# Mixing phase with an early stage eight tiles ahead, 16x16 inverses on VectorE, and the output product in fp16 halves

## Chip, core and metric

One NeuronCore of a Trainium2 chip runs the whole kernel. The metric is the device time of one execution in microseconds. Times inside the run are taken from one profiled execution and count from its first instruction.

## What is computed

The kernel is one inference step of a one-layer encoder over 4096 prompt tokens and 8 running streams of 16 tokens, 33 tiles of 128 tokens in all, D = 1024. A layer is: RMSNorm and one input projection; an RG-LRU group and a gated-DeltaNet group of 4 heads side by side; one output projection and a residual; RMSNorm and a routed mixture of 32 experts (2 per token); a last RMSNorm. The change lies in the DeltaNet group and the output projection:

```python
decay = exp(where(lower, gc[..., :, None] - gc[..., None, :], -inf))
lmat = where(strict, einsum('bhid,bhjd->bhij', k * beta, k) * decay, 0.0)
t_inv = triangular_solve(eye + lmat, eye, lower=True, unit_diagonal=True)
u = t_inv @ (v * beta[..., None])
w = t_inv @ (k * beta * exp(gc)[..., None])
v_new = u - w @ S
o = (q * exp(gc)[..., None]) @ S + (einsum('bhid,bhjd->bhij', q, k) * decay) @ v_new
S_new = S * exp(g_last) + einsum('bhld,bhle->bhde', k * exp(g_last - gc), v_new)
...
mixed = concatenate([out_a, rmsnorm(o, gdn_ng) * silu(z)])
x = x + mixed @ w_out
```

S is carried from tile to tile, so the tiles have an order; t_inv of a tile needs only its own k, beta and decay.

## The kernel before

Five phases run one after the other: projection (all inputs of the mixing go to the DRAM tensor `mixin`), mixing, routing, experts, combine. Only mixing is touched.

Mixing (`mix_phase`) walks over the 33 tiles; the last one holds the streams. The work of a tile is cut into named steps, each on one engine, in three stages: X (what doesn't need S: row sums `stat`, decay `dec`/`DT`, the products `KK` and `QK`, the matrix G, and the inverse of the 128x128 triangle), Y (what needs S: `KS`, `QS`, `X`, `N`, `dS`, `AV`, the head norm `so`/`ro`/`on`, the output product `outA`/`outB`) and R (residual `x2`, second norm `st`/`r2`/`xn`, router `hT`/`lg`/`r0` to `r3`, rank `rk`/`off` and the scatter `sct`).

The list `MIX` (L645 to 669) gives the order by hand: `name.engine` from top to bottom. Each engine runs its own steps in that order (`program`, L799), waiting for the steps it needs by semaphores; one pass of the list does R of tile t, Y of tile t+1 and X of tile t+2, and the loop holds two passes. So a step that waits holds back all that stand behind it on its engine.

The inverse doubles its block size seven times (1, 2, 4, ... 64, `LEVELS`). A level s is: `Bs` on GpSimd (G times a mask), `Ws` on TensorE (L919), `Is` on VectorE (plus identity, L1247), `Ts` on TensorE (L929), its copy `Tsc` on ScalarE (L1070), the transpose `Zs` (L935) and its copy `Zsc` (L1078); level 1 is done on VectorE (`Z1`). Each product is four heads of 128x128 in fp32, which are eight TensorE instructions, a transpose four. The steps `outA0` to `outA3` (two chunks of 128 each, L998) and `outB0` to `outB7` (one head each, L1010) multiply by `w_out` in fp32, 512 columns at a time, and are spread between the levels.

On SP (SyncE's queue) stands one load of the tile's inputs `ft` and one of `xr` per tile (L830, L832). ScalarE issues the stores of x2 and h2, GpSimd the two scatters of `sct` (L1174), each followed by a wait for its landing.

Of the kernel before, what the change touches and what calls it, by code (L numbers as in the profile page):

```python
# [13 lines left out]
FP32 = mybir.dt.float32  # L14
# [24 lines left out]
LEVELS = [1, 2, 4, 8, 16, 32, 64]  # L39
# [4 lines left out]
PROJ = 1.0 / (W_SCALE * H_SCALE)  # L44
G_SCALE = 4.0
# [17 lines left out]
MATS = ["ident", "upto", "after", "upto_s", "after_s", "before", "ones"] + [f"level{s}" for s in LEVELS]  # L63
# [582 lines left out]
X.sq.act X.gs.dve  # L646
Y.KS.pe Y.QS.pe Y.X.dve R.x2.dve Y.o1.act R.st.act R.r2.pool
X.stat.pe X.dec.pe X.sse.dve X.ex.act X.DT.act X.rr.pool R.xn.dve R.h2.pool
Y.N.pe Y.vd.dve Y.vh.act
X.kt.pe X.ktc.act X.vt.pe X.sc.dve  # L650
R.hT0.pe R.hT1.pe R.hc0.dve R.hc1.dve
Y.dS.pe Y.S.dve Y.AV.pe
X.KK.pe X.QK.pe X.vs.act X.G.dve X.B2.pool X.Z1.dve Y.o.dve X.AT.dve
R.lg.pe Y.so.act Y.ro.pool R.r0.dve
Y.outA2.pe X.B4.pool
X.T1.pe X.T1c.act R.r1.dve R.rx.act Y.on.dve
Y.outA3.pe X.ATm.pool
X.W2.pe X.I2.dve Y.outA0.pe
X.T2.pe X.T2c.act Y.outA1.pe Y.oT.pe X.B8.pool
X.W4.pe X.Z2.pe X.Z2c.act Y.mx.dve X.I4.dve Y.outB0.pe X.B16.pool  # L660
X.T4.pe X.T4c.act Y.outB1.pe X.B32.pool
X.W8.pe X.Z4.pe X.Z4c.act R.hh.act X.I8.dve R.r3.dve Y.outB2.pe
X.T8.pe X.T8c.act Y.outB3.pe X.B64.pool
X.W16.pe X.Z8.pe X.Z8c.act X.I16.dve R.hl.dve R.rk.pe
X.T16.pe X.T16c.act Y.outB4.pe R.off.dve
X.W32.pe X.Z16.pe X.Z16c.act X.I32.dve Y.outB5.pe R.sct.pool
X.T32.pe X.T32c.act Y.outB6.pe
X.W64.pe X.Z32.pe X.Z32c.act R.sh.act X.I64.dve Y.outB7.pe
X.Z64.pe X.Z64c.act
# [5 lines left out]
def mix_phase(nc, T, gb, cols, eid, rank, wts, base):  # L675
    NT = tiles()
    H = HEADS
    with ExitStack() as ctx:
# [3 lines left out]
        def sem(name):  # L682
# [3 lines left out]
        w_out = sb("w_out", [P, KD, D])  # L686
# [4 lines left out]
        xr = [sb(f"xr{p}", [P, D]) for p in range(2)]  # L691
        sqb = sb("sqb", [P, 2 * H, P])
# [30 lines left out]
        junk = sb("junk2", [P, D])  # L723
# [75 lines left out]
        def program(engine, begin, x_step, y_step):  # L799

            for (st, e), d in done.items():
                if e == engine:
                    d.begin(begin)

            def run(x, y, r):
                for st, n, e in MIX:
                    tile = {"X": x, "Y": y, "R": r}[st]
                    if e == engine and tile is not None:
                        (x_step if st == "X" else y_step)(n, tile[0], tile[1], tile[2], done[st, e].did)

            last = NT - 1
            run((0, 0, False), None, None)
            run((1, 1, False), (0, 0, False), None)
            with begin.Fori(0, (last - 2) // 2) as pair:
                t = pair * 2
                run((t + 2, 0, False), (t + 1, 1, False), (t, 0, False))
                run((t + 3, 1, False), (t + 2, 0, False), (t + 1, 1, False))
            run((last, 0, True), (last - 1, 1, False), (last - 2, 0, False))
            run(None, (last, 0, True), (last - 1, 1, False))
            run(None, None, (last, 0, True))  # L820
# [1189 lines left out]
```

## Time and profile before

| | us |
|---|---|
| median of 3 runs | 4321.36 |
| lowest, highest | 4320.52, 4328.91 |
| the profiled execution | 4329.62 |
| its span, first to last instruction | 4328.0 |
| TensorE busy | 3577.7 (83%) |
| VectorE busy | 2200.0 (51%) |
| ScalarE busy | 1679.3 (39%) |
| GpSimd busy | 947.6 (22%) |
| mean granted TensorE clock | 0.927 of 2.4 GHz |

A line of the order of time gives the start, the time from the first instruction's start to the last one's end, the engine, the line of the kernel, the operation and its tiles; in brackets how long the engine stood idle before it and who released it. Ends of TensorE instructions are modelled and overlap the next start, so the distance between starts tells what a group occupies. The granted clock is a share of 2.4 GHz; 0.50 is 1.2 GHz.

### The profile page before, as it was taken

The page shows a single profiled execution, that of the slowest core. Times are in us where ns is not written, and L with a number is a line of the kernel's source. Part 1 is how long each engine was busy: PE and PEld are TensorE (multiplying, and loading weights), DVE is VectorE, ACT ScalarE, POOL GpSimd, SP SyncE. Part 2 cuts the span into 40 slices and gives each one's busy share as a digit, 9 for nine tenths or more (in the row PEclk, how much of TensorE's full clock was granted, in tenths as well). Part 3 has the DMA queues.
Part 4 walks back from the last instruction along what each step waited for, and adds up shares of the span by engine and source line. Part 5 has one row for each costly group of instructions (what it writes and reads, how often), then busy time and mean ns, then how long its engine had stood idle before and what let it go on. Part 6 is the DMA issues. An engine that isn't in the chain of part 4 may idle for free. (4 is left out here: it accounts for less than half of the span.)

```text
span 4328.0 us, 72419 instructions
## 1 busy us (share of the span) xinstructions
PE 3577.7 (83%) x21028; PEld 2176.8 (50%) x21029; DVE 2200.0 (51%) x4880; ACT 1679.3 (39%) x2974; POOL 947.6 (22%) x1046
## 2 busy tenths in 40 slices
PE   8987696886978589899989999998739999999920
PEld 3443343333434567666766766676524444444410
DVE  6566474664756445655655565556432222222257
ACT  6556465564655433333333333333112222222222
POOL 0000000000000123333333334333111111111145
PEclk9998898998989699999999999999869999999965
DMA  4465656656565312121112111221046666774379
GB/s 146 150 207 195 223 191 216 213 198 212 196 202 190 131 35 68 53 65 58 63 53 65 58 63 54 64 68 54 15 185 225 224 231 220 271 269 151 107 293 381
DMA packets 293079, 656.24 MB, mean 152 GB/s; under 512 B 26467, under 2 KB 138595, under 8 KB 292579
## 3 DMA queue, kind: packets, MB, share of 16 engines
q1 hardware_dynamic: 182162, 321.70, 23.4%
q0 software_dynamic: 56512, 186.76, 11.5%
q10 hardware_dynamic: 54288, 146.56, 8.7%
q14 instruction: 85, 0.69, 0.1%
q8 instruction: 32, 0.52, 0.1%
HBM read 404.57 MB, written 250.38 MB: 151 GB/s over the span
## 5 line engine op out<-in xcount | busy, mean ns | idle before, releaser
L341 PE MATMUL pP<-h_hi,w_hi 128*128 128x512 f16 (+1 forms) x1728 | 634.8, 371 | 59.4 <-ACT win L435 40.1
L341 PE MATMUL pP<-h_lo,w_hi 128*128 128x512 f16 (+1 forms) x1728 | 634.6, 371 | 0.0
L341 PE MATMUL pP<-h_hi,w_lo 128*128 128x512 f16 (+1 forms) x1728 | 632.8, 370 | 0.0
L1631 PE MATMUL ebank<-ws_sb,rowsT 128*128 x2352 | 528.3, 382 | 40.0 <-issue 39.0
L1631 PEld LDWEIGHTS ebank<-ws_sb,rowsT 128*128 128x128 f16 x2352 | 229.4, 98 | 313.7 <-issue 67.6
L542 DVE SCALAR_TENSOR_TENSOR halves<-stage,halves 128x1024 f16<-128x1024 f32 x192 | 234.5, 1222 | 248.5 <-ACT halves L411 248.5
L293 POOL DMA_DIRECT2D ws<-halves x192 | 103.2, 537 | 1122.1 <-DVE halves L542 615.8
L577 DVE SCALAR_TENSOR_TENSOR cv<-win,cols_sb,cv 128x512 f32<-128x512 f32 (+1 forms) x432 | 305.5, 707 | 33.9 <-issue 0.9
L1247 DVE TENSOR_TENSOR WI<-bank,const 128x512 f32<-128x512 f32 x198 | 136.5, 690 | 351.6 <-PE bank L919 347.1
L341 PEld LDWEIGHTS pP<-h_hi,w_hi 128*128 128x128 f16 x1728 | 174.3, 101 | 256.2 <-ACT win L435 44.6
L411 ACT ACTIVATE halves<-stage 128x1024 f16<-128x1024 f32 x192 | 201.9, 1052 | 259.8 <-POOLq L296 255.7
L1144 POOL TENSOR_TENSOR B<-G,const 128x512 f32<-128x512 f32 x198 | 255.9, 1313 | 139.0 <-DVE G L1228 133.3
L1649 PE MATMUL ebank<-ws_sb,guT 128*128 x1176 | 269.9, 379 | 2.4 <-DVE guT L1705 2.4
L919 PEld LDWEIGHTS bank<-Tm,B 128*128 128x128 f32 x1584 | 196.7, 195 | 146.9 <-ACT Tm L1070 78.4
L1010 PE MATMUL bank<-w_out,mx 128*128 128x512 f32 x528 | 269.6, 594 | 0.8 <-DVE mx L1309 0.8
L341 PEld LDWEIGHTS pP<-h_lo,w_hi 128*128 128x128 f16 x1728 | 174.1, 101 | 190.5 <-issue 19.9
L341 PEld LDWEIGHTS pP<-h_hi,w_lo 128*128 128x128 f16 x1728 | 174.6, 101 | 187.7 <-issue 11.3
L919 PE MATMUL bank<-Tm,B 128*128 128x128 f32 x1584 | 229.9, 290 | 34.6 <-ACT Tm L1066 30.7
L998 PE MATMUL bank<-w_out,ft 128*128 128x512 f32 x528 | 251.0, 599 | 0.0
L929 PE MATMUL bank<-WI,Zm 128*128 128x128 f32 x1320 | 198.1, 295 | 61.5 <-DVE WI L1247 47.6
L929 PEld LDWEIGHTS bank<-WI,Zm 128*128 128x128 f32 x1320 | 167.0, 199 | 156.4 <-DVE WI L1247 84.7
L1700 DVE SCALAR_TENSOR_TENSOR gu<-ebank,sil 128x256 f32<-128x256 f32 x98 | 41.6, 425 | 392.0 <-ACT sil L1668 392.0
(290 smaller groups left out, 6036.3 us busy)
## 6 DMA issues: line engine op xcount, KB each, us to landing
stage<-in_we SPq DMA_DIRECT2D x192, 512.0 KB, 4.1
ws<-halves POOLq DMA_DIRECT2D x192, 512.0 KB, 3.9
ws_sb<-ws SPq DMA_DIRECT2D x32, 3072.0 KB, 13.7
y<-yb ACTq DMA_DIRECT2D x98, 512.0 KB, 4.7
ft<-mixin SPq DMA_DIRECT2D x33, 1280.0 KB, 6.1
mixin<-qo ACTq DMA_DIRECT2D x128, 256.0 KB, 2.8
xt<-in_x SPq DMA_DIRECT2D x33, 512.0 KB, 5.9
xr<-in_x SPq DMA_DIRECT2D x33, 512.0 KB, 4.8
```

The costliest lines, as they stand in the source:

```text
L341: ins = nc.tensor.matmul(pP[n % NPB][:, 0:N], w[:, k, c0:c0 + P], h[:, k, 0:N], start=(k + i == 0), stop=(k == KD - 1 and i == 2))
L411: nc.scalar.activation(halves[:, j % 2, 0, :], stage[:, j % 2, :, :].rearrange("p k n -> p (k n)"), ACT.Copy, scale=W_SCALE).then_inc(expe ...
L542: nc.vector.scalar_tensor_tensor(halves[:, j % 2, 1, :], stage[:, j % 2, :, :].rearrange("p k n -> p (k n)"), W_SCALE, halves[:, j % 2, 0, ...
L577: ins = nc.vector.scalar_tensor_tensor(dst, window(c, j, stream), cw(j), dst, ALU.mult, ALU.add)
L919: ins = nc.tensor.matmul(XB[:, h, :], Bs[s][:, h, :], Tm[:, h, :], start=True, stop=True)
L929: ins = nc.tensor.matmul(XC[:, h, :], Zm[:, h, :], WI[:, h, :], start=True, stop=True)
L998: ins = nc.tensor.matmul(flat((YD, YE)[half]), ft[p][:, QC + ZC + c, :], w_out[:, c, half * 512:half * 512 + 512], start=(c == 0), stop=False)
L1010: nc.tensor.matmul(flat((YD, YE)[half]), mx[:, h, :], w_out[:, LC + h, half * 512:half * 512 + 512], start=False, stop=(h == H - 1)).then_ ...
L1144: nc.gpsimd.tensor_tensor(Bs[s][:, :, :], G[:, :, :], heads(mat(f"level{s}")), ALU.mult).then_inc(*did(n))
L1247: nc.vector.tensor_tensor(WI[:, :, :], XB[:, :, :], heads(mat("ident")), ALU.add).then_inc(*did(n))
L1631: ins = nc.tensor.matmul((M0, M1)[p][:, :], xT[p][:, x, k, :], half(s, k // 2, w, k % 2 * 512), start=(k + i == 0), stop=(k == KD - 1 and ...
L1649: ins = nc.tensor.matmul((OA, OB)[h][:, :], guT[p][:, x, k, :], half(pe_slot[0], W13 // WC + k, w, h * 512), start=(k + i == 0), stop=(k = ...
```

## The change

A fourth stage F is added: `sq`, `gs`, `stat`, `dec`, `KK`, `QK`, G, the scalars `fsc` and the masked `AT` of a tile are made eight tiles ahead (`LEAD`), from q and k loaded on their own (`qk`), and kept in DRAM (`Gs`, `As`, the 16x16 diagonal blocks of G in `Gd`) or in `st_all`. Once in four tiles a step `V` on VectorE inverts the diagonal blocks of four tiles at once: 4 tiles x 4 heads x 8 blocks lie on the 128 partitions (`va`), 15 steps of a product and a subtraction, in two parts in two passes. The results go to DRAM (`Td`, `Zd`) and come back as `Tin` and `Zin`, which GpSimd spreads into block diagonals (`eT`, `eZ`). The levels 1 to 8 go; 16, 32 and 64 stay. The output product takes w_out and both factors as fp16 high and low halves, three fp16 products for one in fp32 (`split_out`, `fh`/`fl`, `mh`/`ml`). A pass now does R of tile i-1, Y of i, X of i+1, F of i+8; the loop holds four passes, from -8 to 33 with those outside the loop.

```diff
 MIX = """
-(18 rows, X, Y and R as above)
+Y.KS.pe Y.QS.pe Y.X.dve R.x2.dve Y.o1.act R.st.act X.eT.pool X.B16.pool X.eZ.pool R.r2.pool
+X.kt.pe X.vt.pe X.sc.dve X.ktc.act F.gs.dve F.sq.act
+Y.N.pe Y.vd.dve Y.vh.act X.vs.act R.xn.dve
+F.stat.pe F.sse.dve F.ex.act F.rr.pool X.B32.pool
+Y.dS.pe Y.AV.pe Y.S.dve
+R.hT0.pe R.hT1.pe R.hc0.dve R.hc1.dve Y.o.dve R.h2.pool
+X.W16.pe X.I16.dve F.dec.pe F.DT.act
+R.lg.pe F.fsc.dve R.r0.dve Y.so.act Y.ro.pool R.hh.act
+X.T16.pe X.T16c.act F.KK.pe F.G.dve X.B64.pool
+Y.outA0.pe X.Z16.pe X.Z16c.act R.r1.dve R.rx.act
+X.W32.pe X.I32.dve Y.outA1.pe Y.on.dve
+X.T32.pe X.T32c.act F.QK.pe F.AT.dve Y.oT.pe F.ATm.pool
+X.Z32.pe X.Z32c.act Y.mx.dve Y.mh.act X.W64.pe X.I64.dve Y.outA2.pe Y.ml.dve
+X.Z64.pe X.Z64c.act Y.outA3.pe R.r3.dve R.sh.act
+Y.outB0.pe Y.outB1.pe R.rk.pe V.v.dve R.hl.dve R.off.dve R.sct.pool
+Y.outB2.pe Y.outB3.pe Y.outB4.pe Y.outB5.pe Y.outB6.pe Y.outB7.pe X.fh.act X.fl.dve
 """.split()
...
+            def early_store(f):
+                sp.wait_ge(*at("G", f))
+                for b in range(NB16):
+                    r = slice(b * BW, (b + 1) * BW)
+                    sp.dma_start(T["Gd"][bass.ds(f, 1), :, b].rearrange("a h i j -> i (a h) j"), G[r, :, r]
+                                 ).then_inc(diag_out, 16)
+                sp.dma_start(T["Gs"][bass.ds(f, 1)].rearrange("a p h n -> p (a h) n"), G[:, :, :]).then_inc(G_out, 16)
+                sp.wait_ge(*at("ATm", f))
+                sp.dma_start(T["As"][bass.ds(f, 1)].rearrange("a p h n -> p (a h) n"), ATf[:, :, :]).then_inc(AT_out, 16)
...
+            def load(t, p, batches):
+
                 sp.wait_ge(*at("mx", t, 2))
                 sp.dma_start(ft[p][:, :, :], T["mixin"][:, :, bass.ts(t, P)]).then_inc(ft_in[p], 16)
-                sp.wait_ge(*at("x2", t, 2))
-                sp.dma_start(xr[p][:, :], T["x"][bass.ts(t, P), :]).then_inc(xr_in[p], 16)
+                sp.wait_ge(*at("B64", t, 1))
+                sp.dma_start(Gin[:, :, :], T["Gs"][bass.ds(t, 1)].rearrange("a p h n -> p (a h) n")).then_inc(G_in, 16)
+                sp.wait_ge(*at("AV", t, 2))
+                sp.dma_start(AT[p][:, :, :], T["As"][bass.ds(t, 1)].rearrange("a p h n -> p (a h) n")).then_inc(AT_in[p], 16)
+                sp.wait_ge(inverse_out, batches * 32)
+                for dst, src, there in ((Tin, "Td", T_in), (Zin, "Zd", Z_in)):
+                    sp.dma_start(dst[p][:, :, :], T[src][bass.ds(t, 1)].rearrange("a h k i j -> (k i) (a h) j")
+                                 ).then_inc(there[p], 16)
...
                 elif n[:-1] == "outA":
...
                     for c in (2 * c0, 2 * c0 + 1):
-                        ins = nc.tensor.matmul(flat((YD, YE)[half]), ft[p][:, QC + ZC + c, :],
-                                               w_out[:, c, half * 512:half * 512 + 512], start=(c == 0), stop=False)
+                        for i, (w, f) in enumerate(((w_out_hi, f_hi), (w_out_lo, f_hi), (w_out_hi, f_lo))):
+                            ins = nc.tensor.matmul(flat((YD, YE)[half]), f[:, c, :],
+                                                   w[:, c, half * 512:half * 512 + 512], start=(c + i == 0), stop=False)
...
+                if n in ("eT", "eZ"):
+                    pool.wait_ge(*at("W16" if n == "eT" else "T16", t, 1))
+                    pool.wait_ge((T_in if n == "eT" else Z_in)[p], ft_turn(t, p))
...
+                    for h in range(H):
+                        ins = nc.gpsimd.tensor_tensor(whole[:, h, :].rearrange("p (k j) -> p k j", k=NB16),
+                                                      small[:, h, :].unsqueeze(1).to_broadcast([P, NB16, BW]), same, ALU.mult)
...
+            def inversion(b, part):
...
+                for k in range(0, 7) if part == 0 else range(7, BW - 1):
+                    n, c = BW - 1 - k, k + 1
+                    prod = vp[:, 0:n * c].rearrange("p (n c) -> p n c", n=n)
+                    nc.vector.tensor_tensor(prod, va[:, k, k + 1:].unsqueeze(2).to_broadcast([P, n, c]),
+                                            vt_[:, k, 0:c].unsqueeze(1).to_broadcast([P, n, c]), ALU.mult)
+                    dve.drain()
+                    nc.vector.tensor_tensor(vt_[:, k + 1:, 0:c], vt_[:, k + 1:, 0:c], prod, ALU.subtract)
+                    dve.drain()
+                if part == 1:
+                    nc.vector.tensor_copy(vz[:, :, :], vt_[:, :, :].rearrange("p i j -> p j i")).then_inc(inverted, 1)
```

`fsc` is today's `sc` with one more copy into `st_all`; X's `sc` becomes one copy out of it. `stat`, `dec`, `KK` and `QK` of F share one PSUM bank, so `stat` of a tile waits for `AT` of the tile before. KS still waits for `off` of two tiles back, which is now among the last steps of the pass before. w_out is loaded in two halves, split on ScalarE and VectorE in the passes -5 and -2.

## Rows read from the trace of the kernel before

**Rows 1.** Windows: stretch, us, busy us (instructions) by engine, clock, DMA share, GB/s.

```profile
1480.00:1530.00 50.00, 37.06 (x175) 32.73 (x174) 11.02 (x29) 10.15 (x19) 11.98 (x9) 0.59 0.36 143
2580.00:2627.00 47.00, 43.52 (x281) 32.75 (x280) 27.43 (x83) 17.04 (x44) 17.32 (x16) 1.00 0.19 61
```

**Rows 2.** Order of time on TensorE, one tile from KS to KS.

```profile
2579.28 1.95 PE L962 MATMUL bank<-S,ft 128*128 128x128 f32 x16
2581.08 2.05 PE L868 MATMUL bank<-const,sqb 128*128 128x128 f32 x16
...
2583.64 1.06 PE L882 MATMUL bank<-const,gs 128*128 128x128 f32 x8
...
2604.42 1.88 PE L998 MATMUL bank<-w_out,ft 128*128 128x512 f32 x4
2606.14 0.60 PE L1005 MATMUL bank<-const,onb 128*128 128x128 f32 x4
2606.58 1.06 PE L919 MATMUL bank<-Tm,B 128*128 128x128 f32 x8
2607.47 0.60 PE L935 MATMUL bank<-const,Tm 128*128 128x128 f32 x4
2607.91 1.02 PE L1010 MATMUL bank<-w_out,mx 128*128 128x512 f32 x2
2608.77 1.15 PE L929 MATMUL bank<-WI,Zm 128*128 128x128 f32 x8
...
2626.26 1.95 PE L962 MATMUL bank<-S,ft 128*128 128x128 f32 x16
```

**Rows 3.** Order of time on TensorE: first stat, first KS, KS of the streams.

```profile
1479.23 3.76 PE L868 MATMUL bank<-const,sqb 128*128 128x128 f32 x16 [20.27 <-ACT sqb L1041]
...
1529.84 1.95 PE L962 MATMUL bank<-S,ft 128*128 128x128 f32 x16
...
3060.74 9.01 PE L959 MATMUL bank<-S_s,kz 128*128 128x128 f32 x64 [3.79 <-DVE kz L1254]
```

**Rows 4.** Order of time on TensorE in the projection, fp16 matmuls of 512 columns.

```profile
1299.75 0.38 PE L341 MATMUL pP<-h_hi,w_lo 128*128 128x512 f16 x1
1299.97 0.38 PE L341 MATMUL pP<-h_hi,w_hi 128*128 128x512 f16 x1
```

**Rows 5.** Order of time on VectorE and ScalarE in the tile of rows 2.

```profile
2582.01 0.68 DVE L1317 TENSOR_TENSOR x2b<-bank,xr 128x512 f32<-128x512 f32 x1
2583.29 1.06 ACT L1108 ACTIVATE junk<-x2b 128x1024 f32<-128x1024 f32 x1 [0.89 <-DVE x2b L1317]
2587.26 2.31 DVE L1214 TENSOR_TENSOR sc<-sse,rr 128x4 f32<-128x4 f32 x1 [0.20 <-POOL rr L1135]
2589.94 0.16 DVE L1220 TENSOR_TENSOR sc<-sc,gt 128x4 f32<-128x4 f32 x1
2590.18 0.16 DVE L1222 TENSOR_TENSOR sc<-sc,ex 128x4 f32<-128x4 f32 x1
2618.87 0.22 DVE L1396 SCALAR_TENSOR_TENSOR offs<-e,r2t 128x1 int32<-128x1 f32 x2
```

**Rows 6.** Order of time on GpSimd in the same tile.

```profile
2587.20 2.35 POOL L1166 TENSOR_TENSOR h2b<-xn,ln_row 128x1024 f32<-128x1024 f32 x1
2603.86 4.95 POOL L1144 TENSOR_TENSOR B<-G,const 128x512 f32<-128x512 f32 x4
2619.93 1.07 POOL L1174 DMA_INDIRECT table<-tid,offs  x1 [11.12 <-DVE offs L1396]
2622.99 0.96 POOL L1174 DMA_INDIRECT table<-tid,offs  x1 [1.99 <-DMA table<-tid,offs]
```

**Rows 7.** Order of time on TensorE, the T2 group after a gap, two tiles.

```profile
1696.82 1.16 PE L929 MATMUL bank<-WI,Zm 128*128 128x128 f32 x8 [2.08 <-DVE WI L1247]
...
1982.28 2.08 PE L929 MATMUL bank<-WI,Zm 128*128 128x128 f32 x8 [2.08 <-DVE WI L1247]
```

**Rows 8.** DMA issues: count, KB each, median us to landing.

```profile
ft<-mixin SPq DMA_DIRECT2D x33, 1280.0 KB, 6.1
```

More of the change, by code:

```diff
@@ L61 @@
 NCOL = _n
-MATS = ["ident", "upto", "after", "upto_s", "after_s", "before", "ones"] + [f"level{s}" for s in LEVELS]
+MATS = ["ident", "upto", "after", "upto_s", "after_s", "before", "ones", "same"] + [f"level{s}" for s in LEVELS]
 NMAT = len(MATS)
@@ L645 @@
 MIX = """
[L646 to L669, printed above, removed]
+Y.KS.pe Y.QS.pe Y.X.dve R.x2.dve Y.o1.act R.st.act X.eT.pool X.B16.pool X.eZ.pool R.r2.pool
[14 more added lines that the diff above has]
+Y.outB2.pe Y.outB3.pe Y.outB4.pe Y.outB5.pe Y.outB6.pe Y.outB7.pe X.fh.act X.fl.dve
 """.split()
@@ L797, in col, with phase, every, tile_at @@
             return cols[:, COLS[name][0] + n:COLS[name][0] + n + w]
-        def program(engine, begin, x_step, y_step):
+        def phase(u):
+            return u // BATCH - 1, u % BATCH
+        last = NT - 1
+        first_loop = 1
+        loops = (last - 1 - LEAD - first_loop + 1) // BATCH
+        def every(engine, iteration):
+            for i in range(-LEAD, first_loop):
+                iteration(i, None)
+            with engine.Fori(0, loops) as four:
+                for u in range(BATCH):
+                    iteration(first_loop + u, four)
+            for i in range(first_loop + loops * BATCH, NT + 1):
+                iteration(i, None)
+        def tile_at(i, four, shift):
+            n = i + shift
+            if four is not None:
+                return four * BATCH + n, n % 2, False
+            return (n, n % 2, n == last) if 0 <= n <= last else None
+        def program(engine, begin, steps, inversion=None, after_first=None):
             for (st, e), d in done.items():
@@ L803, in program, with iteration @@
                     d.begin(begin)
-            def run(x, y, r):
+            def iteration(i, four):
+                if i in (-5, -2) and after_first:
+                    after_first(0 if i == -5 else 4)
+                tiles_ = {st: tile_at(i, four, n) for st, n in (("F", LEAD), ("X", 1), ("Y", 0), ("R", -1))}
                 for st, n, e in MIX:
[L807 to L820, printed above, removed]
+                    if e != engine:
+                        continue
+                    if st == "V":
+                        b, part = phase(i + LEAD)
+                        if part < 2 and (four is not None or 0 <= b <= last // BATCH):
+                            inversion(b if four is None else four + b, part)
+                    elif tiles_[st] is not None:
+                        t, p, stream = tiles_[st]
+                        steps[st](n, t, p, stream, done[st, e].did)
+            every(begin, iteration)
         block = ctx.enter_context(nc.Block())
@@ new lines, in iteration @@
+            def iteration(i, four):
+                whole = lambda n: n if four is None else four * BATCH + n
+                per = lambda n: n if four is None else four + n
+                x, f, nf, nx = (tile_at(i, four, n) for n in (0, LEAD, LEAD + 1, 2))
+                b, part = phase(i + LEAD)
+                valid = four is not None or 0 <= b <= last // BATCH
+                n = 1 if four is None and b == last // BATCH else BATCH
+                if x is not None:
+                    sp.wait_ge(*at("x2", x[0], 1))
+                    sp.dma_start(xr[:, :], T["x"][bass.ts(x[0], P), :]).then_inc(xr_in, 16)
+                if nf is not None:
+                    early_load(nf[0], nf[1])
+                if valid and part == 0:
+                    batch_load(per(b), n, min(whole(i + LEAD), NT) if four is None else whole(i + LEAD))
+                if f is not None:
+                    early_store(f[0])
+                elif four is None and i + LEAD == NT:
+                    sp.wait_ge(G_out, 16 * NT)
+                    sp.wait_ge(AT_out, 16 * NT)
+                if nx is not None:
+                    load(nx[0], nx[1], per((i + 2) // BATCH + 1))
+                if valid and part == 1:
+                    batch_store(per(b), n)
@@ L1188, in _, with f_step @@
         def _(dve):
[L1189 removed]
+            def f_step(n, t, p, stream, did):
                 if n == "gs":
```

363 lines of the change are left out of this document (238 added, 125 removed).

## The prediction

> **What bounds the kernel now.** I read the views from coarse to fine. The windows give the stage: in one steady tile of the mixing phase TensorE is busy 43.5 of 47 us at the full clock (2.4 GHz), VectorE 27.4, ScalarE 17.0, GpSimd 17.3 [rows 1]. The order of time on TensorE then shows why: from one KS to the next is 46.98 us, and the instructions follow each other almost without gaps [rows 2]. Each level of the inverse is W, Z, T with output products filling the waits between them, so here TensorE's own instruction stream sets the end. The mixing tiles run from the first KS at 1529.8 to the KS of the stream tile at 3060.7 [rows 3]; what lies before (projection) and after (routing, experts, combine) is untouched, and I carry it over unchanged. The question is the tile period, the lead-in, and who is late once TensorE has less to do.
>
> **What goes, comes and moves on TensorE.** Occupancy is the distance to the next start [rows 2]: a four-head fp32 group (W, T, dec, KK, QK, N) 0.89; four transposes 0.44; an outA step 1.72; an outB step 0.86; KS with QS 1.80; stat 2.56. Per tile the change removes three W and three T (6 x 0.89 = 5.3), three Z transposes (1.3) and T1 (0.4): 7.1 us. The output product is now 48 fp16 matmuls of 512 columns at 0.22 [rows 4], 10.3 us instead of 4 x 1.72 + 8 x 0.86 = 13.8: 3.4 us less. The rest stays. Adding up the new MIX row by row (KS/QS 1.8, kt/vt 0.9, N 0.9, stat 2.6, dS/AV 1.9, hT 0.9, lg 1.8, the X levels 6.3 with their copies' transposes, dec/KK/QK 2.7, oT 0.4, rk 0.4, outputs 10.3) gives 31 us. That is the floor of a tile, 16 us under today. It is not the forecast, because the engines work in order and the waits no longer hide.
>
> **One tile laid out, without the batched inverse.** I place the steps in MIX order from KS = 0, each at its duration in today's tile (sums in rows 1).
> - KS, QS, kt, vt, N occupy TensorE to 3.6. stat needs sq, and sq now stands on ScalarE behind o1, st and ktc. X and x2 end at 3.5 (0.68 a half [rows 5]); st starts some 0.6 later and takes 1.06 plus its 0.19 read [rows 5]; ktc 0.6 and sq 1.05 end at 7.05. Today sq precedes o1. TensorE idles 3.45 us: a new wait. Behind it queue stat, dS, AV, to 11.5.
> - GpSimd: sct moves to the end of the iteration. After off (which I find 2.4 us before KS) it takes 0.84 to the first scatter [rows 5, 6], 3.06 to the second, and another 3.06 to be free: 4.5 us into the tile. Then eT, B16, eZ stand ahead of r2. B is 1.24 for 512 columns, h2 2.35 for 1024 [rows 6], so 2.1 ns a column and 0.17 fixed: a 128-column piece 0.44, eT and eZ 1.77 each. r2 ends at 10.3 and xn at 11.1: hT follows AV without a wait, barely.
> - hT, W16, dec, then lg behind hc1 to 16.1, T16 and KK to 18.0. VectorE reaches fsc at 15.0, but a two-input instruction in SBUF is held while GpSimd works: today's sc waited 2.31 for a 0.16 operation while h2 ran [rows 5, 6]. h2 runs 14.3 to 16.65 here, so fsc ends at 18.0, r0 at 18.4, and outA0 starts at 18.5. G and r1 (some 13 small steps at the 0.24 spacing of [rows 5]) put I32 at 23.3, so T32 waits 0.9. From there TensorE is dense: QK, oT, Z32, W64, outA2, Z64, outA3 to 30.7, outB and rk to **36.4**. mx, mh and ml (0.7 each) end near 28.8, two us ahead of outB0; they cost nothing as long as on is not late.
>
> **The batched inverse.** Fifteen steps of two VectorE instructions, 30 in all, each with a drain: 0.24 each [rows 5], plus 2 x 680 elements at 1.0 ns (0.68 for 512 against 0.16 for 4), plus two copies of 0.4: 9.4 us per four tiles, in two parts of 4.4 and 5.0. Each part stands between r3 (30.5) and hl, off. hl (1.2) and off (1.45) then end at 37.9 instead of 34, and KS waits for off: 1.5 us. Because sct follows off, r2 of the next tile comes 2.3 us later against its KS, and hT with it. The four tiles of a batch thus take 37.9, 40.2, 38.7, 36.4: mean 38.3.
>
> **Clock.** Of fourteen gaps of 2.08 us ahead of the T2 group eleven were followed by its 1.16 us and three by 2.08, the length at 1.2 GHz (one of each in [rows 7]); after a gap of 3.79 us the 64 instructions of the stream tile's KS took 9.01, where four times the 1.80 of KS with QS is 7.2 [rows 2, 3]. A lost clock thus costs some 1.8 us and comes back within that work. I take it in most tiles at the 3.45 us gap, partly hidden by the wait for xn: 0.9 us a tile, bounds 0 and 1.8. Period **39.2**.
>
> **Transfers.** SP issues 17 DMAs a tile instead of 2. In the order of SP, T and Z go out near 31 and GpSimd wants them at 41. The nearest row is ft: 1280 KB in 512-byte pieces, 2560 of them, lands in 6.1 [rows 8]; T and Z have 512 pieces each, of 64 bytes. I cost them at nothing; each us beyond the 10 of cover would fall on r2. ft itself goes out at 28.5 behind ATm and is wanted at 38, 3 us of cover. The Trainium skill ("DMA: Bandwidth & Descriptors", Specifications) warns that pieces under 512 bytes are not moved at line rate; no row here times a load of 64-byte pieces.
>
> **Lead-in and end.** The first stat starts at 1479.2 and took 3.76 for its first sixteen instructions instead of 1.9: half clock, 0.59 granted over that stretch though TensorE was busy 37 of 50 us [rows 1, 3]. Seven iterations with F alone run serially there: stat 4.75, sse, rr 1.7, fsc beside dec 1.8 and DT 0.6, KK 1.8, G 1.1, QK 1.8, AT 0.7, with hand-overs 14.2 us each: 99. The halves of w_out add some 4, the iteration that adds X(0) 25 (every level at half clock). KS(0) then comes at 1607.6, 78 us later than today. Then 25 tiles with F (980), six without F and its sq, where the r2 chain and the inverse in three of them give about 36 each (216), and 39 for the tile that builds kz: KS of the stream tile at 2843 instead of 3060.7, **218 us earlier**; the shorter output product of the last tile gives 2 more. Against the profiled execution, 4329.6 - 220 = 4110; the median of the runs shown lies 8 below that execution, so **4100**.
>
> **Rivals.**
> *TensorE stays the bound (faster).* If sq and r2 are not late, the tile is its 31 us plus a us of waits. For it: today's stream is that dense. Against it: ScalarE's and GpSimd's order above. 32.5 a tile with F and 32 after gives KS(32) at 2648: 3910.
> *The VectorE-GpSimd hold bites more often.* VectorE gains fsc, ml and 30 two-input instructions, GpSimd eight small ones. Two more holds of 2.15 a tile (the sc row less its own 0.16) are 4.3 x 25 = 108: 4205. Against it: GpSimd waits for off while the inverse runs. The Trainium skill ("SBUF - State Buffer", Who interferes with whom) states this hold as a lock for a whole instruction; the sc row agrees, 2.31 beside h2's 2.35.
> *The clock falls and stays down (slower).* If after the sq gap TensorE stays at 1.2 GHz until outB, the 22 us of work between stat and Z64 take 44; 5 us of gaps absorb part: +17 x 25, 4525. For it: from 1480 to 1530 the granted clock was 0.59 with TensorE busy 37 of 50 us [rows 1]. Against it: the stream tile's KS lost only 1.8 of its 9 us, so the clock came back within it [rows 3]. It decides from 8.8 us a tile, half of that stretch at the low level.
> *The change does not do what it says* would show as W2 to W8 still there; the diff leaves no room.
>
> **How the numbers follow.** Forecast 62 in 100, its own range 4035 to 4170 (period +-2, lead-in +-20); TensorE-bound 15; the hold 15; clock down 6; something near no change 2. Cutting the outer parts of the two faster-than-before rivals leaves 3990 to 4230. Faster by more than 0.2% (9 us, about what a measurement of this kernel can tell from none): 0.91; within: 0.02; slower: 0.07, the clock and a share for a wait not seen.
>
> **What would show it.** Right: KS to KS near 36 to 40 us with a repeat over four tiles; stat preceded by 3 us idle put down to sq; r2 following eZ; the first KS near 1608. Wrong: KS waiting long for off, hT waiting several us for xn in every tile, a clock well under 0.9 between 1610 and 2800, a lead-in over 110 us, or GpSimd waiting for T or Z.

## The result and the profile after

The kernel after takes 4217.5 us (median of four runs, 4215.7 to 4230.0), the kernel before 4321.2 beside it: ratio 0.976 (95% interval 0.974 to 0.978), 104 us faster. The prediction was 4100 us, 220 us faster than the profiled execution of before: the sign is right, the time lies outside the forecast's own range (4035 to 4170) and inside the whole one (3990 to 4230), and the gain is less than half of what was forecast. The profiled execution has a span of 4215.9 us.

The windows of the kernel after (columns as in rows 1): the lead-in stretch, one tile, and twenty tiles.

```profile
1480.00:1530.00 50.00, 31.55 (x170) 27.70 (x169) 23.52 (x75) 10.48 (x15) 10.89 (x7) 0.74 0.27 74
2026.40:2070.00 43.60, 34.63 (x231) 28.64 (x232) 23.51 (x83) 13.91 (x37) 17.46 (x22) 0.92 0.34 102
1700.00:2500.00 800.00, 634.42 (x4272) 519.03 (x4273) 456.74 (x1661) 257.90 (x686) 304.63 (x387) 0.93 0.37 107
```

Where [rows 1] had TensorE busy 43.5 of 47 us at clock 1.00, it is busy 34.6 of 43.6 at 0.92: it has less to do, and it waits. The order of time on TensorE, the same tile (KS to KS, output products left out), shows for whom:

```profile
2026.44 2.02 PE L1094 MATMUL bank<-S,ft 128*128 128x128 f32 x16 [1.70 <-DVE offs L1590]
...
2029.17 1.06 PE L1101 MATMUL bank<-xb,Zf 128*128 128x128 f32 x8
2033.14 3.32 PE L998 MATMUL bank<-const,kz 128*128 128x128 f32 x16 [2.92 <-ACT kz L1177]
...
2038.22 1.06 PE L1121 MATMUL bank<-vhat,AT 128*128 128x128 f32 x8
2043.75 1.85 PE L1153 MATMUL bank<-const,xn 128*128 128x128 f32 x8 [4.48 <-DVE xn L1516]
2045.40 1.92 PE L1049 MATMUL bank<-T,B 128*128 128x128 f32 x8
2047.11 1.17 PE L1013 MATMUL bank<-const,kz 128*128 128x128 f32 x8
...
2057.31 1.15 PE L1061 MATMUL bank<-WI,Zm 128*128 128x128 f32 x8 [1.54 <-DVE WI L1435]
...
2069.99 1.28 PE L1094 MATMUL bank<-S,ft 128*128 128x128 f32 x10
```

Against [rows 2] the tile has gone from 46.98 to 43.55 us (in the mean of the 25 tiles that carry F, from 47.66 to 42.96). The waits for off (L1590), sq (L1177) and the sum with the identity (L1435, the step I32) are those of the layout. The wait of hT for xn, 4.48 us, is not: there it was to follow AV "without a wait, barely". Behind it hT and W16 run at the low clock, 1.2 GHz (1.65 and 1.71 us to the next start, 0.87 and 0.89 at the full clock).

The first KS and the KS of the stream tile, which answer [rows 3], and two instructions of the output product, which answer [rows 4]:

```profile
1609.68 1.95 PE L1094 MATMUL bank<-S,ft 128*128 128x128 f32 x16
...
2956.04 7.31 PE L1091 MATMUL bank<-S_s,kz 128*128 128x128 f32 x64
```

```profile
1679.83 0.38 PE L1144 MATMUL bank<-w_out_hi,mx_hi 128*128 128x512 f16 x1
1680.05 0.38 PE L1144 MATMUL bank<-w_out_lo,mx_hi 128*128 128x512 f16 x1
```

The lead-in ends at 1609.7 (forecast 1607.6). The 25 tiles with F, up to the KS at 2683.79, take 1074.1 us, 42.96 each (forecast 39.2: 94 us of the miss), the six without F, up to the KS at 2916.83, 233 (forecast 216), the one that builds kz 39.2 (forecast 39). The halves of the output product stand 0.22 us apart as assumed.

Why xn is late stands on the three queues around KS at 2026.44. GpSimd:

```profile
2027.05 1.07 POOL L1334 DMA_INDIRECT table<-tid,offs  x1 [11.01 <-DVE offs L1590]
2030.11 0.96 POOL L1334 DMA_INDIRECT table<-tid,offs  x1 [1.99 <-DMA table<-tid,offs]
2037.33 1.68 POOL L1296 TENSOR_TENSOR T<-Tin,const 128x128 f32<-128x128 f32 x4 [6.26 <-DMA table<-tid,offs]
2038.97 1.26 POOL L1304 TENSOR_TENSOR B<-Gin,const 128x512 f32<-128x512 f32 x1
2040.19 1.68 POOL L1296 TENSOR_TENSOR Z<-Zin,const 128x128 f32<-128x128 f32 x4
2041.83 0.18 POOL L1320 TENSOR_TENSOR rs<-s,eps 128x1 f32<-128x1 f32 x1
```

and in the same microsecond ScalarE's store of x2 and SP's loads of xr and qk (its tile is kz), 512 KB each:

```profile
2030.10 0.37 ACTq L1248 DMA_DIRECT2D x<-x2b  x1
```

```profile
2030.10 0.35 SPq L937 DMA_DIRECT2D xr<-in_x  x1
2030.73 1.04 SPq L886 DMA_DIRECT2D kz<-mixin  x1
```

The first scatter kept GpSimd waiting 1.99 us, as in [rows 6]. The second, issued together with 1.5 MB of transfers, kept it 6.26. In a tile without the inverse off comes earlier, and the first scatter has company too. GpSimd and SP ahead of the next KS, at 2069.99:

```profile
2068.64 1.07 POOL L1334 DMA_INDIRECT table<-tid,offs  x1 [7.20 <-DVE offs L1590]
2073.37 0.96 POOL L1334 DMA_INDIRECT table<-tid,offs  x1 [3.66 <-DMA table<-tid,offs]
```

```profile
2062.10 0.57 SPq L918 DMA_DIRECT2D ft<-mixin  x1
2062.95 2.63 SPq L920 DMA_DIRECT2D Gin<-Gs  x1
...
2066.97 0.66 SPq L925 DMA_DIRECT2D Zin<-Zd  x1
```

Here the wait is 3.66 us, and the second scatter meets the store and the loads all the same. eT, B16, eZ and r2 queue behind these waits: at 2041.83 r2 starts 15.4 us into its tile, not some 9.6. From 1700 to 2600 us, over 21 tiles, the waits add up to this (which engine and tile waited for whom; us, times, longest):

```profile
POOL T L1296 <- DMA table<-tid,offs: 106.5, 20, 6.6
PE bank L1153 <- DVE xn L1516: 82.0, 21, 6.6
POOL table L1334 <- DMA table<-tid,offs: 66.3, 21, 4.1
PE bank L998 <- ACT kz L1177: 56.8, 20, 3.1
PE bank L1061 <- DVE WI L1435: 27.3, 21, 1.5
```

### The profile page after: what moved, and what is told of

The parts are those of the page before. It is cut to its first block and busy times, and to the rows that moved or that the text cites. A ratio compares the mean times of both kernels' runs of the same rounds, so it can differ in the third digit from the quotient of the medians.

```text
span 4215.9 us, 68880 instructions
## 1 busy us (share of the span) xinstructions
PE 3265.3 (77%) x19444; PEld 2012.5 (48%) x19445; DVE 2121.2 (50%) x5147; ACT 1585.4 (38%) x2818; POOL 914.9 (22%) x1211
## 5 line engine op out<-in xcount | busy, mean ns | idle before, releaser
L1874 ACT ACTIVATE sil<-ebank 128x256 f32<-128x256 f32 x98 | 37.5, 383 | 390.8 <-PE ebank L1837 390.8
L1516 DVE TENSOR_SCALAR xn<-x2b,rs 128x1024 f32<-128x1024 f32 x33 | 31.1, 944 | 285.9 <-POOL rs L1322 285.9
L334 PE MATMUL pT<-ident,xt 128*128 128x128 f32 x132 | 25.1, 349 | 187.5 <-DVE h_lo L541 173.1
L1153 PE MATMUL bank<-const,xn 128*128 128x128 f32 x264 | 57.1, 387 | 146.0 <-DVE xn L1516 146.0
L1810 POOL DMA_INDIRECT rows<-h,idx x98 | 96.8, 988 | 333.0 <-DMA idx<-table 327.9
L1855 PEld LDWEIGHTS ebank<-ws_sb,guT 128*128 128x128 f16 x1176 | 111.1, 98 | 118.3 <-issue 2.6
L998 PE MATMUL bank<-const,kz 128*128 128x128 f32 x528 | 89.9, 340 | 93.7 <-ACT kz L1177 70.8
L1334 POOL DMA_INDIRECT table<-tid,offs x66 | 67.1, 1017 | 438.7 <-DVE offs L1590 340.5
```

The lines of the kernel that those rows point to most:

```text
L998: nc.tensor.matmul(flat(FB)[:, c:c + P], sqb[:, c, :], mat("ones"), start=True, stop=True)
L1153: ins = nc.tensor.transpose((YD, YE)[half][:, c, :], xn[:, k * P:(k + 1) * P], ident)
L1334: pool.indirect_dma_start(T["table"], bass.IndirectOffsetOnAxis(ap=offs[k][:, 0:1], axis=0), tid[:, 0:1], None).then_inc(ids_out, 16)
L1810: pool.indirect_dma_start(xb[p][:, :, :].rearrange("p h n -> p (h n)"), None, T["h2"], bass.IndirectOffsetOnAxis(ap=idx[p][:, 0:1], axis=0 ...
L1855: ins = nc.tensor.matmul((OA, OB)[h][:, :], guT[p][:, x, k, :], half(pe_slot[0], W13 // WC + k, w, h * 512), start=(k + i == 0), stop=(k = ...
```

## The experiments

Each ran with the kernel before on the same chip; the ratio is to that. The tile is the mean of the 25 tiles with F, KS to KS. T1: the scatters land late because of what runs beside them, and hT is late by that. T2: GpSimd's queue or the landing by itself is slow. T3: the sq gap and the clock set the tile.

| kernel | us | ratio, 95% interval | tile, us |
|---|---|---|---|
| after | 4217.5 | 0.976 (0.974 to 0.978) | 42.96 |
| e1_loads_late | 4154.8 | 0.960 (0.958 to 0.962) | 39.94 |
| e12_store_late | 4125.2 | 0.953 (0.951 to 0.954) | 39.07 |
| e2_no_landing_wait | 4093.8 | 0.946 (0.944 to 0.948) | 38.87 |
| e3_r2_first | 4150.8 | 0.959 (0.958 to 0.961) | 41.12 |
| e4_sq_first | 4228.1 | 0.977 (0.975 to 0.979) | 43.38 |
| e6_no_V | 4164.9 | 0.963 (0.961 to 0.965) | 41.67 |
| e7_fp32_out | 4115.9 | 0.951 (0.950 to 0.953) | 39.80 |
| e10_fp32_no_wait | 4092.1 | 0.946 (0.944 to 0.948) | 39.07 |
| e5_warm | 4089.8 | 0.945 (0.943 to 0.947) | 38.72 |
| e9_warm13 | 4091.9 | 0.946 (0.944 to 0.947) | 38.60 |
| e8_all | 4087.9 | 0.945 (0.943 to 0.947) | 38.64 |
| e11_h2_early | 4091.2 | 0.946 (0.944 to 0.948) | 38.61 |
| e13_warm13_no_V | 4050.7 | 0.937 (0.934 to 0.939) | 37.95 |
| e14_all_fp32 | 4101.7 | 0.948 (0.946 to 0.950) | 39.45 |

### What runs beside the scatter

```diff
 (SP, iteration)
+                if valid and part == 0:
+                    batch_load(...)
+                if f is not None:
+                    sp.wait_ge(*at("G", f[0]))
                 if x is not None:
                     sp.wait_ge(*at("x2", x[0], 1))
                     sp.dma_start(xr[:, :], ...)
                 if nf is not None:
                     early_load(nf[0], nf[1])
-                if valid and part == 0:
-                    batch_load(...)
```

> SP issues the loads of xr and qk behind its wait for G instead of at the start of the tile, so that they no longer run beside the second scatter of sct. Theory T1 (the landing of the scatters is slow because it runs beside SP's bulk transfers, and hT is late by that): GpSimd's wait for table ahead of eT falls from 5.35 us a tile to about 3.1 (the other scatter keeps its 3.2), r2 and xn move forward by 2.2 us, hT waits 1.8 instead of 4.0 us, about 2.2 us a tile or 70 us in all: ratio to the kernel after 0.983, 4150 us. If the landing is slow by itself, whatever runs beside it (T2), GpSimd's wait stays at 5.35 and the time at 4218. If the clock or sq sets the tile (T3), GpSimd's wait may fall but the time stays within 10 us of 4218.

4155 us, as T1 had it, though not by the terms it gave: the tile fell by 3.0 us and not by 2.2, and the lead-in grew by 10. GpSimd's wait and that of hT in the kernel e1:

```profile
POOL T L1298 <- DMA table<-tid,offs: 60.1, 23, 3.5
PE bank L1155 <- DVE xn L1518: 31.0, 18, 2.9
```

The first is 2.6 us a tile, 5.3 in the kernel after; the wait for the other scatter stays (77.7 us in 23 tiles). T2's slow landing falls: the same second scatter lands sooner once two loads stand elsewhere, with the orders of GpSimd and VectorE unchanged.

```diff
-Y.vh.act X.vs.act R.xn.dve
+Y.vh.act X.vs.act R.xs.act R.xn.dve
 (ScalarE; the store leaves st)
+                elif n == "xs":
+                    act.drain()
+                    act.dma_start(T["x2"][bass.ts(t, P), :], x2b[:, :]).then_inc(x2_out, 16)
+                    act.sem_inc(*did(n))
```

> e1_loads_late with the store of x2 also moved, behind vs on ScalarE (some 5 us later), so that nothing large is issued between the second scatter and its landing. T1: GpSimd's wait for the landing ahead of eT falls from 2.6 us a tile in e1 to about 1, the median landing of a scatter from 3.5 us towards the 2.2 us of the kernel before, hT's wait from 1.35 to about 0.4 us: 4155 falls by 20 to 30. If the landing is slow without company, nothing changes: 4155.

30 us less than e1, the upper end of the forecast; GpSimd's wait ahead of eT falls to 42.0 us in 23 tiles, 1.8 (1 was expected). The median time from issue to landing of a scatter between 1700 and 2550 us follows in the same order, in the kernels before, after, e1 and e12:

```profile
table<-tid,offs POOLq DMA_INDIRECT x36, 2.2
```

```profile
table<-tid,offs POOLq DMA_INDIRECT x38, 4.0
```

```profile
table<-tid,offs POOLq DMA_INDIRECT x43, 3.5
```

```profile
table<-tid,offs POOLq DMA_INDIRECT x42, 2.9
```

### Taking the wait off the path

```diff
-R.hT0.pe R.hT1.pe R.hc0.dve R.hc1.dve Y.o.dve R.h2.pool
+R.hT0.pe R.hT1.pe R.hc0.dve R.hc1.dve Y.o.dve R.h2.pool R.scw.pool
 (GpSimd, sct)
-                    pool.wait_ge(ids_out, 32 * t + 32)
                     pool.sem_inc(*did(n))
+                elif n == "scw":
+                    pool.drain()
+                    if not isinstance(t, int) or t:
+                        pool.wait_ge(ids_out, 32 * t)
+                    pool.sem_inc(*did(n))
 (VectorE, off)
-                    dve.wait_ge(*at("sct", t, 1))
+                    dve.wait_ge(*at("scw", t))
```

> GpSimd no longer waits for the landing of the second scatter at the end of sct but behind h2 of the next tile (a new step scw; the loop starts one tile later for it). Theory T1 and T2 alike: the wait of 5.35 us ahead of eT disappears, eT starts some 4 to 5 us into the tile instead of 9.5, r2 ends near 10.5 instead of 15.1, and hT's wait of 4.0 us falls to under 1: the tile goes from 43.0 to about 39.3, that is 25 x 3.7 and 6 x 3 us, some 110 us in all: 4105 us, ratio to the kernel after 0.974. T3 (sq's gap and the clock set the tile): the freed time reappears as waits elsewhere, under 30 us gained.

4094 us and 38.87 us a tile: the forecast of the prediction (4100 and 39.2) is met once this wait is gone. GpSimd of e2, one tile (KS at 2038.60):

```profile
2042.18 0.96 POOL L1334 DMA_INDIRECT table<-tid,offs  x1 [3.92 <-PE bank L1038]
2043.16 1.68 POOL L1296 TENSOR_TENSOR T<-Tin,const 128x128 f32<-128x128 f32 x4
...
2047.67 0.18 POOL L1320 TENSOR_TENSOR rs<-s,eps 128x1 f32<-128x1 f32 x1
```

(PE, the releaser named in the first line, is the profile's inference; by the program the second scatter waits there for the landing of the first.) The second scatter goes out no earlier, but eT follows at once, 4.6 us into the tile, and r2 at 9.1; hT then waits for xn in two tiles of 23. T3 had under 30 us.

```diff
-... R.st.act X.eT.pool X.B16.pool X.eZ.pool R.r2.pool
+... R.st.act R.r2.pool X.eT.pool X.B16.pool X.eZ.pool
```

> On GpSimd r2 stands ahead of eT, B16 and eZ; the scatters and their waits stay. r2 then ends 4.5 us earlier, near 10.6 us into the tile, and W16 gets its inputs as late as before but has hT, dec and lg's copies ahead of it. T1 and T2: hT's wait falls from 4.0 to about 0.5 us; W16 waits for B16 (which ends near 13.4 us, hT near 12.4) for up to 1 us: gain 2.5 to 3.5 us a tile, 4110 to 4140 us. T3: under 30 us gained.

4151 us, less than expected. hT's wait does fall, to 6.1 us in 22 tiles, but outA0 now waits 52.1 us in 22 tiles for the logits, because h2 runs exactly beside fsc. VectorE and GpSimd of e3:

```profile
2074.84 1.22 DVE L1372 TENSOR_TENSOR scf<-sse,rr 128x4 f32<-128x4 f32 x1 [1.34 <-POOL rr L1282]
2075.99 2.38 DVE L1373 TENSOR_TENSOR scf<-rr 128x4 f32<-128x4 f32 x1
2078.29 0.17 DVE L1374 TENSOR_SCALAR scf<-scf 128x4 f32<-128x4 f32 x1
```

```profile
2076.01 2.34 POOL L1326 TENSOR_TENSOR h2b<-xn,ln_row 128x1024 f32<-128x1024 f32 x1
```

Four columns took 2.38 us: the hold of [rows 5], 2.31, in a new place, which is the rival "the hold bites more often" on a small scale.

```diff
-Y.KS.pe Y.QS.pe Y.X.dve ...
+F.sq.act Y.KS.pe Y.QS.pe Y.X.dve ...
-X.kt.pe X.vt.pe X.sc.dve X.ktc.act F.gs.dve F.sq.act
+X.kt.pe X.vt.pe X.sc.dve X.ktc.act F.gs.dve
```

> ScalarE does sq of F at the head of its order instead of behind o1, st and ktc, so that stat finds its operand. T1: the 2.85 us that TensorE waits for sq ahead of stat go, but st comes 1.05 us later only where it is not waiting for x2, hT still waits for xn by way of the late r2, and its wait grows from 4.0 to about 6.5 us: within 20 us of 4218, a little faster where the clock holds up over the shorter gap or slower where it falls over the longer one. T3 (sq's gap sets the tile): 2.85 x 25 = 70 us and the lost clock of some 1 us a tile come back: 4120 to 4150 us.

4228 us, no gain: the waits for sq are gone, and hT waits 164.3 us in 21 tiles, 7.8 instead of 4. The two gaps have become one, and the mean clock from 1700 to 2500 is 0.89 instead of 0.93. T3 falls.

### The parts of the change

```diff
-                for k in range(0, 7) if part == 0 else range(7, BW - 1):
+                for k in ():
```

> The kernel after with the thirty products and subtractions of the batched inverse left out (only its two copies and its transfers stay), so the inverses used are wrong. My layout gave the two halves 4.4 and 5.0 us every fourth tile and, by way of off and of the r2 of the next tile, 1.9 us a tile in the mean: 4218 falls by 30 x 1.9 = 57, to about 4160. If the chain of scatters and r2 sets the tile whatever off does, the gain is under 20 us; if the inverse is hidden beside the output product, none.

53 us by the medians (57 forecast). In the profiled executions it is 60: 1.3 us in each of the 25 tiles (1.9 forecast), 9 us of the lead-in and 20 in the last six tiles.

```diff
-Y.outB2.pe ... Y.outB7.pe X.fh.act X.fl.dve
+Y.outB2.pe ... Y.outB7.pe X.fh.act
 (outA)
-                        for i, (w, f) in enumerate(((w_out_hi, f_hi), (w_out_lo, f_hi), (w_out_hi, f_lo))):
+                        for i, (w, f) in enumerate(((w_out, f_hi),)):
 (outB the same; w_out, f_hi, mx_hi in fp32; ml goes)
```

> The kernel after with the output product in fp32 again: one product for three, the high halves' buffers hold fp32 copies, and the steps fl and ml go. TensorE's output work rises from 48 x 0.215 = 10.3 us to 13.8 us a tile. The outputs lie where TensorE is dense, so my costing gives the whole 3.4 us in 33 tiles, +112: 4330, level with the kernel before. Rival: the wait for r2 and xn sets the tile and only outB (1.7 us) is exposed: +55, 4270.

A plain miss for both theories: 102 us faster, not slower. TensorE's output work did grow by 3.4 us a tile (from 10.6 to 14.0 by the distances between starts), and yet the tile fell from 42.96 to 39.80. GpSimd and the store of x2 in e7, around KS at 2037.29, show why:

```profile
2034.52 1.07 POOL L1331 DMA_INDIRECT table<-tid,offs  x1 [8.39 <-DVE offs L1580]
2038.31 0.96 POOL L1331 DMA_INDIRECT table<-tid,offs  x1 [2.71 <-DMA table<-tid,offs]
2040.77 1.68 POOL L1293 TENSOR_TENSOR T<-Tin,const 128x128 f32<-128x128 f32 x4 [1.51 <-DMA table<-tid,offs]
```

```profile
2040.87 0.37 ACTq L1245 DMA_DIRECT2D x<-x2b  x1
```

outB2 to outB7 behind off are longer, so that the first scatter goes out 2.8 us ahead of KS in the tiles without the inverse (after: 1.35) and the second 1.0 us into the tile, 2.6 ahead of the store and loads, and has landed when they start. In 24 tiles of e7 it was issued at 0.6 to 2.8 us and eT started at 3.0 to 7.2; in 24 of after at 3.1 to 4.5, and eT at 7.3 to 11.3. The output product was the cover of the scatter. (e7 also spares VectorE fl and ml, 0.7 us each. In the tiles without the inverse the first scatter moves by 1.41 us against KS, and the stretch on TensorE from the start of rk's last product to KS, which holds outB2 to outB7, grows by 1.35, from 4.11 to 5.46: there nearly all of the shift is the product's. In the tiles with the inverse the parts were not separated.)

```diff
 (e7_fp32_out and e2_no_landing_wait together)
```

> e7_fp32_out and e2_no_landing_wait together. In e7 the second scatter goes out 1.0 us after KS, ahead of the store of x2 and the loads of xr and qk, and hT waits 0.25 us for xn. T1: the landing is no longer on the path there, so the wait taken away brings nothing: 4105 to 4116, and the product in fp16 is worth 10 to 20 us without the landing wait (4094 against this) where it cost 102 us with it. If the landing wait still costs as in the kernel after, another 60 to 120 us go: 4000 to 4050.

4092 us, 24 less than e7 and level with e2. The wait thus still cost e7 something: in one tile of four (the 5th, 9th, 13th and 17th behind the first KS) its second scatter went out at 2.3 to 2.8 us and eT waited 3.2 to 3.5. With e7 it makes a square: the fp16 halves cost 102 us with the landing wait (4217.5 against 4115.9) and neither cost nor bring anything without it (4093.8 against 4092.1).

### What sets the tile once the landing wait is gone

```diff
 (e2_no_landing_wait; TensorE, stat)
                     pe.wait_ge(*at("AT", t, 1))
+                    if not isinstance(t, int) or t >= LEAD:
+                        for _ in range(20):
+                            nc.tensor.matmul(flat(FB)[:, 0:P], mat("ones"), mat("ones"), start=True, stop=True)
                     pe.wait_ge(*at("sq", t))
```

> The kernel e2_no_landing_wait with TensorE kept busy in the gap ahead of stat: twenty fp32 products of ones by ones, 128 columns each, some 2.2 us at full clock, into the bank that stat then overwrites, from tile 8 of F on. In e2 the gap for sq is about 3.1 us a tile and the 16 instructions of stat behind it took 3.07 to 3.66 us where a warm stat takes 1.9. If the gap costs the clock, stat falls back to 1.9 us, the granted clock between 1700 and 2500 rises from 0.95 to about 1.00, and 24 tiles lose 1.2 to 1.6 us each: 4094 falls to 4055 to 4065. If stat is slow for another reason, nothing changes (4094). If the extra products outlast the gap, the time rises by what they overrun, up to 20 us.

4090, level with e2. The clock came back (0.99 from 1700 to 2500 us, where e2 has 0.95), and stat with it (1.8 to 2.0 us in every tile, where e2 has 2.0 to 3.6), here one tile of e2 and one of e5:

```profile
2045.23 3.07 PE L998 MATMUL bank<-const,kz 128*128 128x128 f32 x16 [2.92 <-ACT kz L1177]
```

```profile
2045.21 4.63 PE L996 MATMUL bank<-const 128*128 128x128 f32 x40
2049.67 1.95 PE L1001 MATMUL bank<-const,kz 128*128 128x128 f32 x16
```

but the products took 4.5 us, more than the gap, which gave it away again. So they were cut to thirteen:

```diff
-                        for _ in range(20):
+                        for _ in range(13):
```

> As e5_warm with thirteen products instead of twenty. In e5 each product occupied 0.23 us (two instructions), 4.66 us in all where the gap was 3.27, so what the clock gave back (stat 3.31 to 1.88 us, its second part 1.02 to 0.74) went into the overrun. Thirteen occupy 3.0 us and fit the gap. If the clock costs 1.7 us a tile in e2, the time falls from 4094 by some 24 x 1.5 = 36 to about 4057. If VectorE and GpSimd set the 38.7 us that e2, e5 and e8 share, it stays at 4090.

4092. The gain of the clock did not reach the end here either: in the mean of twenty tiles KS waited 0.83 us (e2: 0.77), stat's second part 0.75 for gs (0.42), hT 0.22 (under 0.05), outA0 0.34 (0.11), and the tile became 0.3 us shorter.

```diff
 (e1_loads_late, e2_no_landing_wait, e3_r2_first and e4_sq_first together)
```

> All four moves together: no wait for the second scatter's landing at the end of sct, loads of xr and qk behind G, r2 ahead of eT, B16 and eZ, sq at the head of ScalarE's order. The sq gap of 3.1 us a tile and its clock loss go only if hT then finds xn ready: st ends 5.3 us into the tile, r2 6.4, xn 7.4, and hT follows AV at 8.2. Then the tile is some 35 us against 39.0 in e2: 25 x 4 and 6 x 1, 4094 falls to about 3990. If r2 stays tied to the landing of the first scatter, or outA0 waits for the logits as it does in e3 (2.4 us a tile), 4030 to 4050.

4088, 6 below e2, which is not clear of the noise (the ratios to before are 0.943 to 0.947 and 0.944 to 0.948): sq's gap has gone, and outA0 waits 2.2 us a tile for the logits, W16 1.2 for B16, hT 0.7 for xn.

```diff
 (e8_all)
-... R.r2.pool X.eT.pool X.B16.pool X.eZ.pool
+... R.r2.pool X.eT.pool X.B16.pool R.h2.pool R.scw.pool
-F.stat.pe F.sse.dve F.ex.act F.rr.pool X.B32.pool
+F.stat.pe F.sse.dve F.ex.act F.rr.pool X.eZ.pool X.B32.pool
```

> e8_all with h2 on GpSimd directly behind B16 (while VectorE works on operands in PSUM) and eZ behind rr. In e8 outA0 waited 2.2 us a tile for the logits, because two small operations of fsc were held for 1.2 and 2.4 us beside GpSimd's rr, B32 and h2. If that hold sets the tile, outA0's wait falls under 0.5 us and the tile from 38.6 to about 36.5: 4088 falls to 4030. If the first scatter and r2 set it, 4088 stays.

4091: the wait for the logits is gone, and T16 waits 1.8 us a tile for eZ instead.

```diff
 (e9_warm13)
-                for k in range(0, 7) if part == 0 else range(7, BW - 1):
+                for k in ():
```

> e9_warm13 with the thirty operations of the batched inverse left out (the inverses used are then wrong). e2, e5, e8, e9 and e11 all take 38.6 to 38.9 us a tile whatever was taken off TensorE's waits. If VectorE sets that (busy 72 of 100 us in e9), the mean of 2.4 us a tile that the inverse occupies comes back nearly whole: 4092 falls by 25 x 2 = 50 to about 4040. If TensorE's stream with its other waits sets it, only the wait of KS for off goes (0.44 us a tile): under 15 us.

4051, between the two expectations. Of the 38 us between the two profiled executions, 12 are lead-in, 16 the 25 tiles (0.65 each) and 9 the six without F: in the steady tiles a quarter of VectorE's 2.4 us reaches the end.

```diff
 (e8_all, with the output product of e7_fp32_out)
```

> e8_all with the output product in fp32 (as e7). In e10 TensorE's only waits are 3.0 us for sq and 0.45 for the identity sum; 34.4 us of work and these make its 38.9 us. If TensorE sets e10, sq first and r2 first take up to 3 us and the lost clock: 36 to 37 us a tile, 4092 falls to 4030. If VectorE and GpSimd set the tile here as in e8 (outA0 waiting 2.2 us for the logits, W16 1.2 for B16), the outputs in fp32 come on top of those: 4090 to 4120.

4102: outA0 waits 2.7 us a tile for the logits, W16 0.7 for B16; TensorE's gaps at sq are gone and its tile is no shorter than e10's.

What single loop sets these 38.6 to 39.5 us stays open. What is shown is that a wait taken from one place turned up at the next. That several loops end within a microsecond of each other there (TensorE's 31 us with the sq gap; fsc and the logits behind rr and h2; off behind the inverse) is the reading of it, and was not shown loop by loop.

## Why the prediction went as it did

**Right.** TensorE's floor and the durations of its groups, the sq gap (2.8 us a tile for 3.45), the wait for the sum with the identity (1.3 for 0.9), and, among the signs of being wrong, hT's wait for xn in every tile. Without the landing wait the forecast of the time and of the tile holds (e2: 4094 us, 38.87 a tile), with two terms that make up for each other: hT waits 0.2 us a tile for 1.1, and the clock takes 1.3 for 0.9.

**Right in the sum only, by luck.** The lead-in (1609.7 for 1607.6) is a sum of errors that cancel. The first stat starts 7.8 us earlier than the 1479.2 that it was counted from, the stretch of the seven iterations with F alone, up to X(0), takes 118 us where 99 and 4 for w_out were laid out, and the iteration with X(0) 21 for 25:

```profile
1471.39 3.78 PE L998 MATMUL bank<-const,kz 128*128 128x128 f32 x16 [18.78 <-DVEq L1605]
...
1589.03 1.11 PE L1033 MATMUL bank<-const,ft 128*128 128x128 f32 x4 [9.73 <-DMA ft<-mixin]
```

The inverse cost 53 us in all for 57, but 1.3 us in each of the 25 tiles for 1.9, with 9 in the lead-in, where the sum had none, and 20 in the last six.

**The step that failed** is that on GpSimd: sct "takes 0.84 to the first scatter, 3.06 to the second, and another 3.06 to be free: 4.5 us into the tile", with the paragraph on transfers that costs them "at nothing". The row under it was of a kernel whose first scatter had no other transfer beside it. The first scatter went out where it was laid out, 1.35 us ahead of KS in the tiles without the inverse (1.6 forecast), but GpSimd then waited 3.6 us for it, beside ft, Gin, AT, Tin and Zin; the second, at 3.1 to 4.5 us instead of 1.5, met the store of x2 and the loads of xr and qk, and kept GpSimd 5.3 us in the mean. eT thus started at 7.3 to 11.3 us, mostly above 9.3, instead of 4.5, and hT, which was to follow "barely", waited 3.9 us a tile (82.0 in 21 tiles). e2 gives the price of the wait for the second scatter: 124 us, against 117 us by which the forecast was missed. That the second scatter's wait comes of its company is shown by e1, e12 and e7, which move one or the other party and leave the wait in the program. For the first scatter's 3.6 us it is argued only: no run moved the five loads ahead of it.

The prediction checked T, Z and ft for their own lateness, and not what they and the loads of x and of q and k would do to a small transfer beside them, which somebody waits for on an engine in order. The Trainium skill ("DMA: Bandwidth & Descriptors", Queues, rings and completion order) has the rule that would have asked that: SP's and ScalarE's queues are rings on the same 16 engines, and a completion count lands only after every earlier write of that engine, across its queues. The rows agree as far as they go, 2.2 us in the kernel before and 4.0 in the kernel after in the median; whether shared engines or the order of the writes make the difference, no run here tells. (The scatter itself goes out on GpSimd's queue, of which that passage does not speak.)

**The clock** was a second term too small. I took 0.9 us a tile, with bounds of 0 and 1.8; the groups between stat and lg lose 2.5 us in the mean against the same groups in e5 (stat 2.42 for 1.88, its second part 1.02 for 0.74, hT 1.45 for 0.88, the rest no more than that each). There were two gaps, at sq and at xn, instead of one; in e2, which keeps only that at sq, the same groups lose 1.3. With the extra wait for xn this is the tile's excess, in the 17 tiles from 1772 to 2506 us: 2.4 at xn (3.5 there, 1.1 in the layout) and 1.6 of clock, less 0.6 at sq, plus 0.4 at the sum with the identity and 0.2 at KS for off, make 4.0, and 43.2 less 39.2 is 4.0. e4 and e9 show that the clock's part is not a cost by itself: it follows the waits, and returned without a wait being removed it brings little.

**The output product** was costed as 3.4 us a tile saved on TensorE. The saving is there, and it is worth nothing (e2 against e10) or less (after against e7): TensorE did not set the end any more, and its own work was what gave the scatter time to land. The prediction priced this edit by the engine that bounded the kernel before.

**Rivals.** The hold between VectorE and GpSimd was not what made the kernel slower than forecast (VectorE was busy 457 of 800 us, and 579 in e2, which is faster), though e3 shows it. TensorE as the bound did not come: 31 us of work in 43. The clock falling for good did not come.

## What to carry to other kernels

Before a wait for a small transfer is moved, look at what else is issued in the same microseconds, on all queues: its price is set by its company, not by its row in the old place. When the bound engine is relieved, every us saved on it can also be taken from the cover of whatever its queue hid, as here; price each part of a change against the chain that will be late, not against the engine that was. And where several loops end within a us of each other, as they seem to here at 38.7, one more wait removed may only name the next.

## What was not expected of the hardware

The wait for a scatter of 128 numbers grew from 2.0 us to 6.3 when 1.5 MB were issued in the same microsecond. And behind gaps of mostly 2.9 us the 16 instructions of stat took 1.9 us in ten of 23 tiles of the kernel after and 2.3 to 3.6 in the others, while the kernel without the landing wait, with TensorE kept busy on useless products through that gap, ran at a clock of 0.99 to 1.00 from 1700 to 2500 us (0.95 without them) and ended no sooner.
